# Two mixture-of-experts stages: 32-column units and eight weight slots in the first, three fixed experts in both, first pass formed before the ranking

## The reference, cut to what matters

```python
def grouped_moe(h, router_w, router_b, w_gate, w_up, w_down):
    scores = sigmoid(hf @ router_w)                    # (t, 16)
    biased = scores + router_b
    # best group of four experts (sum of its two best), then the two best experts in it
    wsel = wsel / sum(wsel)
    for e in range(16):
        u = silu(hf @ w_gate[e]) * (hf @ w_up[e])      # 1024 -> 512
        out = out + combine[:, e:e + 1] * (u @ w_down[e])   # 512 -> 1024
```

## Time and profile before

| | us |
|---|---|
| median of three runs | 1373.3 |
| span of the profiled execution | 1372.4 |
| PE busy in it | 1304.7 (95%) |
| DVE, ACT, POOL busy | 562.7, 375.3, 206.9 |
| first product of moe0 to its last | 603.7 to 863.7 |
| first product of moe1 to the last store's issue | 1132.2 to 1368.0 |

### The profile page before, as it was taken

The page is one execution under the profiler, slowest core; times in us unless marked ns, Lnnn a source line. Parts: engine busy times, 40 slices in busy tenths (PEclk is TensorE's granted clock), DMA queues, the critical chain, the costliest instruction groups (busy, mean ns, idle before and its releaser), DMA issues.

```text
span 1372.4 us, 14111 instructions
## 1 busy us (share of the span) xinstructions
PE 1304.7 (95%) x5515; PEld 631.4 (46%) x5515; DVE 562.7 (41%) x934; ACT 375.3 (27%) x718; POOL 206.9 (15%) x198
## 2 busy tenths in 40 slices
PE   5899999999999999989999999999999889999996
PEld 3444445444444445564344343444445475444442
DVE  1457456565474232542111111753419472222213
ACT  2335656667567000100010000320127211000000
POOL 1001334434334200010000000311102200000001
PEclk9999999999999999999999999999999999999999
DMA  9233665675756630579999999940000759999997
GB/s 360 89 127 123 215 239 186 251 260 201 268 173 237 237 121 28 228 269 362 428 427 428 427 429 405 378 167 0 1 16 0 283 210 397 362 428 429 428 427 287
DMA packets 76652, 354.37 MB, mean 258 GB/s; under 512 B 9401, under 2 KB 27497, under 8 KB 61217
## 3 DMA queue, kind: packets, MB, share of 16 engines
q1 hardware_dynamic: 67643, 326.16, 60.4%
q10 hardware_dynamic: 5564, 15.16, 2.9%
q0 software_dynamic: 3376, 12.12, 2.5%
HBM read 339.51 MB, written 13.90 MB: 258 GB/s over the span
## 4 chain that ended last, share of the span: by engine, by line
PE 79%; DMA 8%; DVE 6%; ACT 2%; issue 1%; ACTq 1%; SPq 1%; POOL 0%; POOLq 0%; DVEq 0%
PE psum L1638 25%; PE psum L2323 10%; PE psum L771 10%; PE psum L782 8%; PE psum L1116 6%; DMA ring<-in_moe_w_up 4%; PE psum L299 3%; PE psum L1697 2%; PE psum L2375 2%; PE psum L259 2%; PE psum L815 2%; PE psum L835 1%; DMA moe_y_d<-arena 1%; DMA arena<-mod_d 1%; PE psum L831 1%
## 5 line engine op out<-in xcount | busy, mean ns | idle before, releaser
L1638 PE MATMUL psum<-ring,arena 128*64 128x512 f32 (+1 forms) x1344 | 400.6, 596 | 9.8 <-DMA ring<-in_moe_w_up 3.2
L1638 PEld LDWEIGHTS psum<-ring,arena 128*64 128x64 f32 (+1 forms) x1344 | 144.3, 151 | 230.4 <-issue 213.6
L771 PE MATMUL psum<-hT,ring 128*128 128x512 f32 x384 | 169.7, 596 | 0.0
L2323 PE MATMUL psum<-ring,hT 128*128 128x512 f32 x320 | 138.9, 593 | 0.0
L1116 PE MATMUL psum<-ring 128*128 128x512 f32 x256 | 112.1, 595 | 2.1 <-ACT ring L930 1.3
L771 PEld LDWEIGHTS psum<-hT,ring 128*128 128x128 f32 x384 | 71.4, 190 | 91.3 <-issue 91.3
L782 PE MATMUL psum<-hT,ring 128*128 128x512 f32 x256 | 112.5, 592 | 0.0
L976 DVE SCALAR_TENSOR_TENSOR arena<-arena,cols 128x512 f32<-128x512 f32 x96 | 92.8, 966 | 3.4
L2323 PEld LDWEIGHTS psum<-ring,hT 128*128 128x128 f32 x320 | 60.1, 190 | 72.9 <-issue 72.2
L1822 DVE TENSOR_TENSOR arena<-arena,psum 128x512 f32<-128x512 f32 x20 | 21.0, 1052 | 136.0 <-PE psum L1638 136.0
L914 ACT ACTIVATE ring<-ring,dts 128x128 f32<-128x128 f32 x256 | 76.5, 387 | 0.5
(11 more groups left out here) (353 smaller groups left out, 1574.4 us busy)
## 6 DMA issues: line engine op xcount, KB each, us to landing
ring<-in_moe_w_down SPq DMA_DIRECT2D x30, 2048.0 KB, 19.3
ring<-in_moe_w_gate SPq DMA_DIRECT2D x28, 2048.0 KB, 19.2
ring<-in_moe_w_up SPq DMA_DIRECT2D x26, 2048.0 KB, 17.2
arena<-in_ada_w SPq DMA_DIRECT2D x60, 512.0 KB, 5.9
ring<-in_ssd_w_in SPq DMA_DIRECT2D x16, 1024.0 KB, 7.2
ring<-acs_d SPq DMA_DIRECT2D x16, 1024.0 KB, 6.8
ring<-in_da_w_in SPq DMA_DIRECT2D x6, 2048.0 KB, 18.2
ring<-in_ada_w SPq DMA_DIRECT2D x20, 512.0 KB, 4.7
```

The lines of the kernel that those rows point to most:

```text
L771: mm = pe.matmul(psum[:, bank, :], w_[:, k, c0:c0 + P], hT[:, k, :], start=(k == 0), stop=(k == KD - 1))
L1638: mm = pe.matmul(psum[rows, dst, :], lhsT[:, k, rows], slot(s_, a)[:, k, part], start=(k == 0), stop=(k == a - 1))
L2323: mm = pe.matmul(psum[:, 4 + m_ % 2, :], hT[:, k, t * P:(t + 1) * P], slot(qkv_slot[n], KD)[:, k, :], start=(k == 0), stop=(k == KD - 1))
```

## The change: what it does, and the diff

1. `moe0` is cut in units of 32 columns. An expert has 64, 96 or 128 columns, and a lane of a rank may be split over two passes. There are 10 passes. Where all lanes of a pass are multiples of 64 it still runs as 64-wide matmuls; in the passes of (96, 32) and (96, 32) columns each k-step has four matmuls of 32 stationary columns. `moe1` keeps 9 passes with 64 or 128 columns.
2. `moe0` uses eight slots. The weights of the first pass's down product go to slots 6 and 7; the first waits until the four blocks of `moe_h_d` are stored, the second until the router's logits are done. A slot is taken again in the order in which slots fall free.
3. Three experts are fixed (`NPRE = 3`). In `moe0` the first pass is that of the experts 1 and 2, in `moe1` that of 0 and 1, with 64 columns each. Its mask is formed from the counts alone, before the ranking: four DVE instructions, then in `moe0` eight matmuls with one column for the token list of pass 0 (line 1455 of the new kernel), a copy, and the gather; in `moe1` a fifth DVE instruction and the selection at once. The list for the other passes follows in `index_tensor`, behind the transposes of pass 0. The loads of rank 3 and up still wait for the ranking.
4. The semaphore for the transposed tokens counts halves, and a gate product starts on the first half. The ranking tables have two rows instead of three, and `place_vector` computes row numbers once.

The diff, cut to its core:

```diff
-        NPRE = 2
-        M_READY, AB_READY = 1, 2
+        NPRE = 3
+        UNIT = 32
...
+                keep = phases.index((G - 2, 2)) if nt == TT else len(phases)
+                    if i < len(slots):
+                        s_ = slots[i]
+                    else:
+                        f = next(freed)
+                        while self.place[f][0] >= SLOTS and closed[u_][0] > keep:
+                            f = next(freed)
+                        s_, self.after[u_] = self.place[f][0], f
...
             def router_tensor(self, pe):
-                keep_busy(pe, 5, 30)
-                pe.wait_ge(s["route_done"], at["route_done"] + AB_READY)
+                if self.first:
+                    keep_busy(pe, 5, 12)
+                    return
+                keep_busy(pe, 5, 15)
+                pe.wait_ge(*self.routed("FIRST"))
+                for t in range(nt):
+                    for e in range(2):
+                        m = pe.matmul(psum[:, 7, 0:1], self.onehot_0[:, 2 * t + e, :], self.tokf[:, t:t + 1],
+                                      start=(t + e == 0), stop=(t == nt - 1 and e == 1))
+                m.then_inc(s["rank_mm"], 1)
+                keep_busy(pe, 5, 40)
+
+            def index_tensor(self, pe):
+                pe.wait_ge(*self.routed("AB"))
                 for n in range(2 * nt):
-                    m = pe.matmul(psum[:, 6, 256:256 + self.ng], self.onehot_s[:, n, :], self.onehot_g[:, n, :],
+                    m = pe.matmul(psum[:, 7, 128:128 + self.ng], self.onehot_s[:, n, :], self.onehot_g[:, n, :],
...
             def place_vector(self, v, step):
+                a0 = slice(self.static, self.static + 2)
+                step(stt(out=self.bad, in0=place[:, :, a0], scalar=64.0, in1=self.m[:, :, a0], op0=ALU.is_ge, op1=ALU.is_ge))
+                step(tt(out=self.sv, in0=place[:, :, a0], in1=self.many(self.tab[:, 3, NE - 2:NE], nt), op=ALU.add))
+                step(stt(out=self.sv, in0=self.bad, scalar=1000.0, in1=self.sv, op0=ALU.mult, op1=ALU.add))
+                if self.first:
+                    step(tt(out=first2[0], in0=self.many(self.iota128, 2 * nt), in1=over(sv, P), op=ALU.is_equal))
+                    tt(out=first1[0], in0=first2[0][:, 0:2 * nt:2, :], in1=first2[0][:, 1:2 * nt:2, :], op=ALU.add).then_inc(s["route_done"], 1)
+                else:
+                    tt(out=self.onehot_0, in0=self.many(self.iota128, 2 * nt), in1=over(sv, P), op=ALU.is_equal).then_inc(s["route_done"], 1)
...
+                if not self.first:
+                    v.wait_ge(s["rank_mm"], at["rank_mm"] + 2)
+                    v.tensor_copy(self.idx[:, 0:1], psum[:, 7, 0:1]).then_inc(s["route_done"], 1)
...
             def router_pool(self, pool):
                 for j in range(2):
                     pool.wait_ge(self.row_stored[j], self.at["rows"][j] + 16 * (nt // 2))
-                pool.wait_ge(s["route_done"], at["route_done"] + self.IDX_READY)
+                if not self.first:
+                    pool.wait_ge(*self.routed("IDX0"))
...
             def gathers(self, pool):
                 for n in range(self.first, self.ng):
+                    if n == 1:
+                        pool.wait_ge(*self.routed("IDX"))
...
             def product(self, pe, n, m, dst, lhsT, part=slice(0, NB)):
-                ranks = self.groups[n]
-                width = P // len(ranks)
+                lanes = self.groups[n]
+                tile = P if len(lanes) == 1 else 64 if all(w_ % 64 == 0 for _, _, w_ in lanes) else UNIT
                 for k in range(a):
-                    for lane, r in enumerate(ranks):
+                    if m == 0 and k % (KD // 2) == 0:
+                        name = "hgT_b" if k else "hgT_a"
+                        pe.wait_ge(self.s[name], self.at[name] + n + 1)
+                    for r, col, width in lanes:
...
-                        rows = slice(lane * width, (lane + 1) * width)
-                        mm = pe.matmul(psum[rows, dst, :], lhsT[:, k, rows], slot(s_, a)[:, k, part], start=(k == 0), stop=(k == a - 1))
+                        for c0 in range(col, col + width, tile):
+                            rows = slice(c0, c0 + tile)
+                            mm = pe.matmul(psum[rows, dst, :], lhsT[:, k, rows], slot(s_, a)[:, k, part], start=(k == 0), stop=(k == a - 1))
...
         moe0 = Moe("moe0", 0, range(TT),
-                   ((0,), (1, 15), (2,), (7, 8), (3,), (9, 10), (4,), (11, 12), (5,), (13, 14), (6,)),
-                   (4, 5, 0, 1, 2, 3), (2, 2, 1, 1, 2, 2), None, None, (nA, nS, ngb, nh, njunk))
+                   (((1, 2), (2, 2)), ((0, 3), (5, 1)), ((5, 2), (8, 2)), ((3, 4),), ((6, 3), (7, 1)), ((7, 2), (9, 2)), ((4, 4),),
+                    ((10, 2), (11, 2)), ((12, 2), (13, 2)), ((14, 2), (15, 2))),
+                   ((0, 1), (0, 2), (1, 1), (1, 2), (0, 0), (1, 0), (2, 1), (2, 2)),
+                   (4, 5, 0, 1, 2, 3, 6, 7), (2, 2, 1, 1, 2, 2, 0, 0), None, None, (nA, nS, ngb, nh, njunk))
...
-                   ((0, 1), (2,), (4, 5), (6, 7), (8, 9), (10, 11), (3,), (12, 13), (14, 15)),
+                   (((0, 2), (1, 2)), ((2, 2), (5, 2)), ((3, 4),), ((6, 2), (7, 2)), ((8, 2), (9, 2)), ((4, 4),),
+                    ((10, 2), (11, 2)), ((12, 2), (13, 2)), ((14, 2), (15, 2))),
...
+            moe0.sync_first(sp, SLOTS, (stored, [moe0.scored()]))
...
+                                    [(A["out_added"], 4), (norm_s["sumsq"], moe1.norm.at["sumsq"] + LT)], [moe1.scored()]))
```

More of the change, by code:

```diff
@@ L1216, in expand, with __init__ @@
             return v.rearrange("p a (b o) -> p a b o", o=1).broadcast_to([P, v.shape[1], v.shape[2], n])
-        NPRE = 2
-        M_READY, AB_READY = 1, 2
+        NPRE = 3
+        UNIT = 32
         class Moe:
-            def __init__(self, tag, layer, tiles, order, slots, fills, before, norm_before, norm_bufs):
+            def __init__(self, tag, layer, tiles, order, ahead, slots, fills, before, norm_before, norm_bufs):
                 self.bank = 7 if len(tiles) == TT else 4
@@ new lines, in place_vector @@
+                if self.first:
+                    self.tokens_mask(v, step, 1)
+                else:
+                    ohg = self.onehot_g
+                    step(tt(out=ohg, in0=self.past[:, :, 0:G], in1=self.past[:, :, 1:G + 1], op=ALU.subtract))
+                    ohg4 = ohg.rearrange("p (k t) g -> p k t g", k=2)
+                    tok4 = self.tokf.rearrange("p (o t u) -> p o t u", o=1, u=1).broadcast_to([P, 2, nt, G])
+                    step(tt(out=ohg4, in0=ohg4, in1=tok4, op=ALU.mult))
+                    tt(out=self.onehot_s, in0=self.many(self.iota128, 2 * nt), in1=over(self.slotv, P), op=ALU.is_equal).then_inc(s["route_done"], 1)
@@ L1564, in place_vector @@
+                w2 = self.w.rearrange(flat)
+                step(v.tensor_reduce(out=w2, in_=self.prod, axis=AX.X, op=ALU.add))
                 step(tt(out=self.ws, in0=self.w[:, 0, :], in1=self.w[:, 1, :], op=ALU.add))
@@ L1605, in weights, with sync_first @@
                 return w_.rearrange("o (p k) n -> p (o k) n", p=P), (KD, KD, KE)[m]
-            def sync_first(self, sp, waits):
-                for i in range(SLOTS):
-                    for w_ in waits[i]:
+            def sync_first(self, sp, first, waits):
+                for i, waits_ in enumerate(waits, first):
+                    for w_ in waits_:
                         sp.wait_ge(*w_)
@@ L1615, in sync_rest @@
             def sync_rest(self, sp):
-                sp.wait_ge(self.s["route_done"], self.at["route_done"] + self.PERM_READY)
-                expert = {}
-                for i in range(SLOTS, 3 * NE):
-                    m, r = self.seq[i]
+                expert = {r: r for r in range(NPRE)}
+                for m, r in self.seq[len(self.slots):]:
+                    if len(expert) == NPRE:
+                        sp.wait_ge(*self.routed("PERM"))
                     if r not in expert:
@@ L1823, in gated_ @@
                                     in1=psum[:, 3, :].rearrange("p (q k) -> p q k", k=KE), op=ALU.mult).then_inc(s["u_ready"], 1)
-                if not self.first:
-                    tokens(0)
-                if self.first > 1:
-                    self.tokens_mask(v, step, 1)
                 tokens(1)
```

214 lines of the change are left out of this document (108 added, 106 removed), and 1 row of the table moe1.

## The result

| | before | changed |
|---|---|---|
| median, us | 1373.57 (1373.19 to 1377.93, 4 runs) | 1358.59 (1352.48 to 1368.32, 4 runs) |
| ratio | | 0.9886 [0.984, 0.9931] |
| span of the profiled execution | 1372.4 | 1355.4 (it took 1357.08 in all) |
| mean granted clock in it | 0.992 | 0.987 |

The change makes the kernel faster by 15 us, where 28 were forecast; 1358.6 lies outside the range of 1336 to 1354. The four runs of the changed kernel lie 15.8 us apart, so the prediction's "tells changes over 0.2%" is too fine for it; even the fastest, 1352.5, is 7 us above the forecast. The two traces are best compared from landmark to landmark: the counting matmul (L1415, now L1445), the first combining matmul of moe0 (L1747, now L1800), the first gate product.

What follows compares the result with a forecast made beforehand. The prediction took moe0 as close to balance, the weight stream slightly ahead as limit, and moe1 as limited by PE. 1372.4 - 19.3 (moe0) - 8.5 (moe1) = 1344.6 on the profiled span, said as 1345, range 1336 to 1354.

Steps and rivals of the forecast that it cites:

- The stream in moe0: moe0's weight loads: two loads ahead of before, last weights landing at 837.1 against 848.2.
- The head of moe0: moe0, start of pass 0: gather takes 10.5, first gate product starts at 605.0 and ends 1.3 later than before.
- The 32-column products: Six products in two moe0 passes: 0 to 4 us extra on PE, taken as 0; the skill's figure gave 11.
- its down product needs both, and takes 7.0: 844.1: End of moe0: the last pass's down product follows the last weights and ends at 844.1, against 863.7 before.
- the lead of 15.5 us: End of moe0: the last weights landed 15.5 us before PE's end; the forecast said this lead goes.
- moe0's term: Gain of moe0 up to its sums, forecast at -19.3 us.
- the other chain: End of moe0: down 8, its store, gathers and sums, ending at 845 where it gave 864.1.
- moe1's term: Head of moe1: first gate product at 1123.7 instead of 1132.2, carried to the end: -8.5 us, bounds -6 and -11.
- Rival 1: Head of moe0: the early gather takes 5.1, the gate starts at 599.8, kernel 1338; chance 0.2.
- rival 3: 32-column matmuls run two by two: 42 us more on PE, 12 idle, kernel 1375; chance 0.03.
- rival 4: An expert overflows its columns and the fallback runs, over a millisecond; chance 0.01.
- Rival 2: Later moe0 head or lower clock, 32-column steps costing 4 to 11, or moe1's mask late: 1352 to 1358; chance 0.15.

Runs made afterwards that it cites:

- e1: Changed kernel with the modulation's three small loads issued before moe0's remaining weight loads instead of behind them: 1350.86 us, ratio 0.9812.
- e4: e1 with moe0 in 11 passes without 32-column products, eight slots kept: 1369.71 us, ratio 0.9961.
- e9: e6 with keep_busy behind moe1's counts cut from 12 to 8 matmuls: 1346.34 us, ratio 0.9775.
- e8: e3 with moe1's first selection waiting for pass 1's mask, behind the ranking, and keep_busy of 30 matmuls again: 1359.55 us, ratio 0.9882.
- e3: e1 with the loads into slots 6 and 7 issued only after the gather of pass 0 has landed: 1348.75 us, ratio 0.9789.
- e7: e1 with six slots in moe0 instead of eight: 1359.76 us, ratio 0.9893.
- e10: e1 with moe0's early token list undone, so pass 0's gather waits for the list of all passes: 1362.01 us, ratio 0.9888.
- e6: e3 with keep_busy ahead of moe1's counts raised from 10 to 19 matmuls: 1347.60 us, ratio 0.9817.

## Why the prediction was wrong, point by point

- **The stream in moe0** was right in its causes: without the two loads the stage is 10.0 longer. The last weights landed at 837.4 (forecast 837.1). That the two agree so closely is in part luck, for from the counts it is 1.8 later than forecast.
- **The head of moe0** was right in place, with the terms a little large: the gather took 8.9 (10.5 taken), the gate product 7.1 (8.6 taken; `keep_busy` lasted to 598 and not to 595, and PE then stood still for 1.2 us). What I had as "up to 2 us more" for the second gather became 4.4 of waiting and a stretch at the lower clock. Sum nearly right, 18.9 against 20.5 to the first gate product.
- **The 32-column products** were right at cost 0: 7.07 us each. The Trainium skill (TensorE: Matmul & The Clock Gate, Part 3: Packing small matmuls — row/col tiling) measured 2.38x for three column tiles of 32. The share of full packing that I took from it is not what four tiles show here: a k-step takes 0.88 us, as with two tiles of 64, and the 11 us worked out from it did not come. No run here has three tiles.
- **The step that failed** is "its down product needs both, and takes 7.0: 844.1". I had seen that the lead of 15.5 us goes, but only for the weights. The same lead had covered what stands behind the last weight load in SP's order, and I put that at nothing. These five loads are issued 12.5 us earlier in the changed kernel, yet the transpose that reads three of them could come some 20 us earlier (at 833 instead of 854) and had to wait until 841. The down product started 5.8 us after its weights had landed (843.2 against 837.4) and took 2.65 longer at the lower clock. It ended at 852.9 instead of 844.1. Moving the small loads gives back 6.1 of the 9.5 us by which the term was too large (e1).
- **The other 3.4 us of moe0's term** are a size in the other chain. I had it at 845, 260.5 us after the counts; in e1 it ends the stage at 263.7, since down 8 ended 2.9 later than forecast. The 844.8 of e1's trace looks like my 845 only because its counts came 3.4 us sooner. PE also had less idle time than I had put (about 8 us and not 12, an estimate from e4).
- **moe1's term** had the right mechanism and was mis-sized: 6.2 instead of 8.5. The mask came as forecast, 2.9 after the counts; the forecast let PE take it at once, but PE was in `keep_busy` at the lower clock for 2.2 us more. e9 has the head of 6.45 that I had forecast (1123.7 - 1117.24 = 6.46, the counts from the trace of before). That the term is carried to the end in full was right (e8, by its trace).
- **Rest**: +1.55 between the stages, -1.5 before and -1.0 behind, not forecast. I have not tried what makes them; the start alone varies by more than this from one execution to the next.
- **Rivals.** Rival 1 (a quick gather: 8.9 us and not 5.1) and rival 3 (32 columns two by two: 7.07 us a product and not 13 or more) did not come, nor did rival 4. Rival 2 was nearest in time (1352 to 1358), and names a lower clock after waits of the last passes, but the wait itself is not among its causes.

## What to carry to other kernels

When a change takes away the lead that one product had over a stream, list everything that is issued in the same queue behind the last item of that stream, and who waits for it: small loads can land as late as the big ones that are queued ahead of them (26.1 us here), and what was hidden by the lead is now on the path. Issue what the next stage needs before the stream, not behind it. Filling an engine with empty work to hold its clock has to be judged on both sides: in moe1 a gap of 2.35 us ahead of the counts let the clock fall, and then the empty matmuls behind them took longer than the wait that they were to fill.

## What the runs showed of the hardware

- Four 32-column matmuls of 512 moving columns in f32 into four row groups of PSUM take 0.88 us a k-step, the same as two of 64 columns (changed kernel, 7.07 and 7.09 us for eight k-steps).
- A load of 4 KB took 26.1 us to land behind the queued 2 MB loads of SP (changed kernel).
- A gather of 512 KB took 8.5 to 8.9 us whether two further 2 MB loads had just been queued (the changed kernel, e1) or not (e3, e7), and 10.8 when it was issued 17.9 us after the counts, with those two still in the queue (e10).
- The granted clock went to 0.50 while PE stood still for 7.7 us (changed kernel). In moe1's head it fell after 2.35 us of standing still that followed a mix of small matmuls; with that gap filled to 0.33 us it stayed at 1.00 (e6). How long the same 24 records took behind the gap varied from one execution to the next, 4.25 to 5.47 us.
